# All taps of six channel tiles of a depthwise convolution on TensorE, as four output phases on 32-row blocks

## The reference

```python
TAPS = 31                                  # CONV_A_WIDTH; D_MODEL = 1024, SEQ = 512
def mixer_conformer_conv(x, w_pw1, b_pw1, w_dw, b_dw, ln_g, ln_b, w_pw2):
    a, g = jnp.split(x @ w_pw1 + b_pw1, 2, axis=-1)
    h = a * jax.nn.sigmoid(g)
    h = causal_depthwise_conv(h, w_dw) + b_dw       # 31 taps, one filter per channel
    h = jax.nn.silu(layer_norm(h, ln_g, ln_b))      # over the 1024 channels
    return h @ w_pw2
...
x = layer_norm(ALPHA * x + h, ln1_g[i], ln1_b[i])   # then a SwiGLU FFN, a second norm,
                                                    # and a gated per-layer embedding
```

## Time and profile before

| | |
|---|---|
| median of 3 runs | 2545.72 us (2544.5 to 2546.34) |
| the profiled execution's own time | 2546.59 us |
| its span | 2544.8 us |
| TensorE matmuls busy | 2520.1 us, 99% |
| TensorE weight loads busy | 2314.1 us, 91% |
| VectorE busy | 1955.3 us, 77% |
| ScalarE busy | 1200.0 us, 47% |
| mean granted TensorE clock | 0.999 |

### The profile page before, as it was taken

The page is one execution under the profiler, slowest core; times in us unless marked ns, Lnnn a source line. Parts: engine busy times, 40 slices in busy tenths (PEclk is TensorE's granted clock), DMA queues, the critical chain, the costliest instruction groups (busy, mean ns, idle before and its releaser), DMA issues. The chain is left out here.

```text
span 2544.8 us, 41246 instructions
## 1 busy us (share of the span) xinstructions
PE 2520.1 (99%) x17241; PEld 2314.1 (91%) x17241; DVE 1955.3 (77%) x2571; ACT 1200.0 (47%) x1960; POOL 1.4 (0%) x10
## 2 busy tenths in 40 slices
PE   9999999999999999999999999999999999999999
PEld 7899999889888899998898899998898999999888
DVE  6988999577454679995784479996677979999576
ACT  6775444436233254443362245444356766444335
POOL 0000000000000000000000000000000000000000
PEclk9999999999999999999999999999999999999999
DMA  5202333324322223333233224333222203333322
GB/s 156 73 12 92 113 103 108 103 88 128 95 92 91 84 89 103 107 101 108 82 101 97 94 67 123 103 108 107 92 91 93 66 26 97 103 107 102 108 82 76
DMA packets 267054, 240.10 MB, mean 94 GB/s; under 512 B 14908, under 2 KB 212852, under 8 KB 266740
## 3 DMA queue, kind: packets, MB, share of 16 engines
q1 hardware_dynamic: 266292, 236.94, 30.2%
q10 hardware_dynamic: 576, 0.52, 0.1%
HBM read 233.21 MB, written 2.10 MB: 92 GB/s over the span
## 5 line engine op out<-in xcount | busy, mean ns | idle before, releaser
L1786 DVE TENSOR_TENSOR w_lo<-raw,w_hi 128x1024 fp32r<-128x1024 f32 x287 | 345.4, 1222 | 266.0 <-ACT w_hi L1309 265.7
L1309 ACT CAST w_hi<-raw 128x1024 fp32r<-128x1024 f32 x287 | 294.8, 1045 | 372.8 <-DMA raw<-in_ffn_w_down_dram 104.1
L879 PE MATMUL psum<-h_hi,w_lo 128*128 128x512 f32 x872 | 341.4, 392 | 0.0
L881 PE MATMUL psum<-h_hi,w_hi 128*128 128x512 f32 x872 | 339.4, 389 | 0.0
L880 PE MATMUL psum<-h_lo,w_hi 128*128 128x512 f32 x856 | 333.2, 389 | 0.0
L1024 PE MATMUL psum<-a_hi,w_lo 128*128 128x256 f32 x1088 | 280.9, 286 | 6.6 <-DVE w_lo L1786 5.1
L1024 PE MATMUL psum<-a_hi,w_hi 128*128 128x256 f32 x1088 | 277.5, 284 | 0.0
L1190 PE MATMUL psum<-h_hi,w_hi 128*128 128x256 f32 x768 | 217.3, 283 | 0.0
L1191 PE MATMUL psum<-h_hi,w_hi 128*128 128x256 f32 x768 | 217.3, 283 | 0.0
L1024 PEld LDWEIGHTS psum<-a_hi,w_lo 128*128 128x128 f32 x1088 | 209.1, 192 | 8.7 <-DVE w_lo L1786 4.6
L1024 PEld LDWEIGHTS psum<-a_hi,w_hi 128*128 128x128 f32 x1088 | 209.3, 192 | 0.3
(11 more groups left out here) (362 smaller groups left out, 6494.3 us busy)
## 6 DMA issues: line engine op xcount, KB each, us to landing
raw<-in_ffn_w_gate_dram SPq DMA_DIRECT2D x176, 256.0 KB, 3.0
raw<-in_ffn_w_up_dram SPq DMA_DIRECT2D x176, 256.0 KB, 3.3
raw<-in_ffn_w_down_dram SPq DMA_DIRECT2D x176, 256.0 KB, 3.1
raw<-in_a_w_pw_dram SPq DMA_DIRECT2D x94, 256.0 KB, 3.1
raw<-in_ple_w_gate_dram SPq DMA_DIRECT2D x64, 256.0 KB, 3.2
raw<-in_b_w_in_dram SPq DMA_DIRECT2D x64, 256.0 KB, 3.0
raw<-in_c_w_in_dram SPq DMA_DIRECT2D x48, 256.0 KB, 2.9
raw<-in_b_w_out_dram SPq DMA_DIRECT2D x32, 256.0 KB, 3.1
```

Of the source, the lines that this page charges most:

```text
L879: pe.matmul(bank(grp.g, j), st_lo, mv_hi, start=(k == 0), stop=False, skip_group_check=by_tiles(grp))
L881: done = pe.matmul(bank(grp.g, j), st_hi, mv_hi, start=False, stop=(ku == last and a == UK - 1), skip_group_check=by_tiles(grp))
L1309: act.copy(hi_u[u % RING], raw_u[u % RING]).then_inc(hi_ready, 1)
L1786: dve.tensor_tensor(lo_u[u % RING], raw_u[u % RING], hi_u[u % RING].bitcast(F32), ALU.subtract)\
```

## The change

TensorE makes all 31 taps of six tiles (2 to 7); VectorE keeps tiles 0 and 1. Four output phases take the place of two: a matmul has 32 rows and 128 output columns (32 channels by four phases), the four row groups r go to four PSUM banks, and 31 taps and four phases give 34 steps. Tiles 2 to 5 are made over all 512 tokens (128 moving columns for each matmul); tiles 6 and 7 in two halves of the tokens (64 moving columns), in the order 6 and 7 of half 0, 6 and 7 of half 1. Successive segments alternate between the two halves of PSUM. The DMAs that moved quadrants are gone: ScalarE (`move`) and VectorE (`move_half`) copy 32-partition pieces out of PSUM, 16 copies by ScalarE for a whole tile, eight by each engine for half a tile. ScalarE makes the blocks of tiles 2 and 3, VectorE those of tiles 4 to 7 (`make_blocks`). The full diagonals, the taps of tiles 2, 3 and 7 on VectorE and the two ScalarE starts (`conv_begin`) are gone.

```diff
-PHASED = ((4, 0), (5, 0), (3, K_SHARED), (6, 0))
-TILE_ROWS = P // 2
+PHASES = 4
+ROWS = P // PHASES
+STEPS = TAPS_A + PHASES - 1
+QUADS = (2, 3, 4, 5, 6, 7)
+ACT_BLOCKS = 2
+A_BLOCKS = 3
+SEGMENTS = ((0, None), (1, None), (2, None), (3, None), (4, 0), (5, 0), (4, 1), (5, 1))
+CENTRE_IN, CENTRE_AT = 3, 20
+STATS_AT = 18
...
+        def moves(s, i, groups):
+            n, (v0, n_v) = SEGMENTS[i][0], segment_span(i)
+            y = by_phase(tiles(h_f32, CONV_Y + QUADS[n]))
+            return [(rows(y, r)[:, PHASES - 1 - j, v0:v0 + n_v], rows(segment_bank(s, i, r), j))
+                    for r in groups for j in range(PHASES)]
...
-            def phase_tap(s, n, e):
-                at = e % 2 * (CW // 2) + e // 2
-                for w, x in ((0, 1), (1, 0), (0, 0)):
-                    for r in range(2):
-                        moving = conv_split(n, x)[r * TILE_ROWS:(r + 1) * TILE_ROWS, at:at + HALF]
-                        last = pe.matmul(phase_bank(s, n, r)[:, 0:HALF], block_pair(n, e, w, r), moving, ...)
+            def quad_tap(s, i, e):
+                n, (v0, n_v) = SEGMENTS[i][0], segment_span(i)
+                at = e % PHASES * (CW // PHASES) + e // PHASES + v0
+                for w, x in ((0, 1), (1, 0), (0, 0)):
+                    for r in range(PHASES):
+                        moving = rows(conv_split(n, x), r)[:, at:at + n_v]
+                        block = rows(tap_blocks(n, w), r)[:, e * ROWS:e * ROWS + P]
+                        last = pe.matmul(segment_bank(s, i, r), block, moving, ...)
...
             def conv_taps(s):
+                for i, (n, h) in enumerate(SEGMENTS):
+                    if i < 2:
+                        take_half(s.taps_g + i)
+                    else:
+                        pe.wait_ge(moved_high, moved(s, i - 2))
+                        pe.wait_ge(moved_low, moved(s, i - 2))
+                    if i == CENTRE_IN + 1:
+                        pe.wait_ge(centre_saved, c + 1)
...
+                    for e in range(STEPS):
+                        last = quad_tap(s, i, e)
+                        if i == CENTRE_IN and e == CENTRE_AT:
                             centre(s)
+                        if i == len(SEGMENTS) - 1 and e == STATS_AT:
+                            conv_stats(s, 0)
                     last.then_inc(taps_done, 1)
...
             # ScalarE
+            def move(s, i):
+                act.wait_ge(taps_done, moved(s, i))
+                for y, out_of in moves(s, i, HIGH):
+                    last = act.copy(y, out_of)
+                last.then_inc(moved_high, 1)
+                if i < WHOLE:
+                    for y, out_of in moves(s, i, LOW):
+                        last = act.copy(y, out_of)
+                    last.then_inc(moved_low, 1)
...
             def conv_norm(s):
+                for i in (4, 5):
+                    move(s, i)
+                    conv_half_square(s, i)
+                move(s, 6)
+                load_sqrt()
+                half_moments(s, 0)
+                half_root(s, 0)
+                move(s, 7)
+                load_silu()
+                conv_half_square(s, 6)
+                half_affine_pair(s, 0, 0)
...
             # VectorE
+            def make_blocks(s, n):
+                if n >= A_BLOCKS:
+                    dve.wait_ge(pe_done, s.groups[-1].end())
+                m = QUADS[n]
+                for part in range(2):
+                    ...
+                    last = dve.tensor_tensor(three(tap_block(n, 0, part, TAPS_A), TAPS_A), many(rep[:, :], TAPS_A),
+                                             taps.broadcast_to([P, TAPS_A, ROWS]), ALU.mult)
+                last.then_inc(blocks_made, 1)
+            def move_half(s, i):
+                m, h = QUADS[SEGMENTS[i][0]], SEGMENTS[i][1]
+                dve.wait_ge(taps_done, moved(s, i))
+                for y, out_of in moves(s, i, LOW):
+                    last = dve.tensor_copy(y, out_of)
+                last.then_inc(moved_low, 1)
+                wait_moved(s, i)
+                place_centred(s, m, h)
...
             def conv_norm(s):
+                move_half(s, 4)
+                add_half(s, 4)
+                add_half_square(s, 4)
...
+                half_root(s, 0)
+                half_scale(s, 0, 0)
+                half_scale(s, 0, 1)
+                move_half(s, 7)
+                add_half_square(s, 6)
+                add_half(s, 7)
+                half_lo_pair(s, 0, 0)
```

More of the change, by code:

```diff
@@ L381, in tap_block @@
[L381 to L401, removed]
+            return ap.rearrange("p (q v) -> p q v", q=PHASES)
@@ L403, in prm_taps, with mean_bank, square @@
+        def mean_bank(s):
+            return bank(s.taps_g, 0, 2).rearrange("p (h s) -> p h s", h=2)[:, :, SEQ // PHASES:SEQ // PHASES + HALF]
+        SQUARES = DT + TILES
+        def square(m):
+            return tiles(a_f32, SQUARES + m - TILES)
         def prm_taps(s):
@@ L943, in last_tap @@
[L943 to L948, removed]
+                    for r in range(PHASES):
+                        moving = rows(conv_split(n, x), r)[:, at:at + n_v]
+                        block = rows(tap_blocks(n, w), r)[:, e * ROWS:e * ROWS + P]
+                        last = pe.matmul(segment_bank(s, i, r), block, moving, start=(e == 0 and (w, x) == (0, 1)),
+                                         stop=(e == STEPS - 1 and (w, x) == (0, 0)))
@@ L1902, in phase_add @@
-            def phase_add(s, n):
-                dve.wait_ge(phase_turned[n], 64 * (s.layer // 3 + 1))
-                own.settle()
-                y = by_phase(tiles(h_f32, CONV_Y + PHASED[n][0]))
-                own.add(dve.tensor_tensor(y, y, phased(turned(n)[1]), ALU.add))
-            def make_shared_blocks(s, part):
-                dve.wait_ge(pe_done, s.groups[-1].end())
-                m, n = PHASED[SHARED][0], TAPS_A - K_SHARED
-                taps = (taps_lo if part else prm_taps(s)).rearrange("p (k m) -> p k m", m=DT)[:, K_SHARED:TAPS_A, m:m + 1]
-                to = (h_hi, h_lo)[part][:, SHARED_AT + TILE_ROWS:SHARED_AT + (n + 1) * TILE_ROWS]
-                dve.tensor_tensor(three(to, n), many(rep, n), taps.broadcast_to([P, n, TILE_ROWS]), ALU.mult)\
-                   .then_inc(shared_blocks, 1)
@@ new lines, in add_half, with add_half_square @@
+            def add_half(s, i):
+                c, m, h = s.layer // 3, QUADS[SEGMENTS[i][0]], SEGMENTS[i][1]
+                last = i % 2 == 1
+                dve.wait_ge(z_ready, Z_READY * c + i + 2)
+                own.settle()
+                ins_ = dve.tensor_tensor(hcol(tiles(tmp, 5), h), hcol(tiles(tmp, 5), h), hcol(conv_tile(m), h), ALU.add)
+                ins_.then_inc(conv_sums, 1) if last else own.add(ins_)
+            def add_half_square(s, i):
+                c, m, h = s.layer // 3, QUADS[SEGMENTS[i][0]], SEGMENTS[i][1]
+                last = i % 2 == 1
+                dve.wait_ge(sq_ready, 7 * c + i)
@@ L2254, in convolve @@
                         lo_to(min(lo_end[0] + 1, lo_end_at))
-                    for m in (m0, m0 + 1) if k > first or not begun else ():
+                    for m in (m0, m0 + 1):
                         x = conv_x[:, m, PAD - taps + 1 + k:PAD - taps + 1 + k + SEQ]
@@ L2265, in convolve @@
                             own.add(dve.scalar_tensor_tensor(y, x, w, y, ALU.mult, ALU.add))
-            def tap_alone(s, m, k, y, fresh=False):
-                x, w = conv_x[:, m, k:k + SEQ], col("a_w_dw", s.layer // 3 * TAPS_A + k, m)
-                if fresh:
-                    own.add(dve.tensor_scalar(y, x, w, None, ALU.mult))
-                else:
-                    own.add(dve.scalar_tensor_tensor(y, x, w, y, ALU.mult, ALU.add))
-            def convolve_alone(s, m, first, end):
-                sums = tiles(h_f32, CONV_Y + m), tiles(tmp, 5)
-                for k in range(first, end):
-                    own.settle(back=1)
-                    tap_alone(s, m, k, sums[(k - first) % 2], fresh=(k == first + 1))
-                own.settle()
-                own.add(dve.tensor_tensor(sums[0], sums[0], sums[1], ALU.add))
             def gated_input(s, grp):
```

419 lines of the change are left out of this document (169 added, 250 removed).

## The result

The changed kernel takes 2712.73 us (median of 4 runs, 2710.82 to 2716.29) against 2545.11 us (2543.06 to 2546.34): a ratio of 1.0661, 95% interval 1.0643 to 1.068, or 167.6 us more. The profiled execution's span is 2709.0 us. The time lies in the range of the prediction and the direction is the one forecast; of the loss of 167.6 us the prediction had 76.

What follows compares the result with a forecast made beforehand. TensorE's matmuls, busy 99% of the span, were taken to bound the kernel. Two layers by (34.4 + 3.8) = 76.4 us on the profiled 2546.6 gave 2623.0, set at 2622 us as that execution was 0.9 above the median; range 2598 to 2740.

Steps and rivals of the forecast that it cites:

- Added on TensorE: Tap stages: 816 groups of four 32-row matmuls at 119.2 ns, 97.3 us, 34.4 us more than before in each layer.
- the same for 128 and for 64 columns: Sign expected in the new trace's taps: groups of four every 110 to 120 ns at either stream length.
- almost full clock: Reading of the profile before the change: TensorE's matmuls busy 99% of the span at nearly the full clock.
- The load bounds the group: Taps: if four row groups load and stream at once, the 128-column weight load sets a group's price, 109 to 119.2 ns.
- bounds 109 and 119.2: Price of a tap group in ns: bare distance between loads, and price of a 64-row pair, which was taken.
- The tail: Behind the taps: ScalarE's copies, table load and square before the first SiLU, 3.8 us of new TensorE idle time per layer.
- upper bound of 6.6 us: Most that the new idle time behind the taps could be; the least was 1.9 us.
- What was costed at nothing: VectorE's changed work, segments' waits for inputs, sums and banks, ScalarE's whole-tile copies and removed quadrant DMAs: no added time.
- The faster one: Rival for the taps: quarter-height loads faster or hidden, the stream decides; 16.5 us saved per layer, 2513 us; chance 0.13.
- Short streams at plain float32's rate: Rival for the taps: float32r under 256 columns about fourfold slower, 225 ns for 128 columns; 2708 us; chance 0.07.
- Slow instructions: Rival for the taps: eight instructions per group bound it, 2715 us at 22 ns each, up to 2817; chance 0.22.
- the likeliest case: Whole kernel: the forecast of load-bound groups plus idle time behind the taps, 2602 to 2634 us; chance 0.56.

Runs made afterwards that it cites:

- e1: The changed kernel with the half segments streaming all 128 columns, half of their results unused; 2637.1 us, ratio 1.0366.
- e10: The changed kernel with 32 unused words more, so later tensors lie where they lay before the change; 2690.8 us, ratio 1.0575.
- e6: On top of e5, tiles 3 to 6 run two passes as one 256-column matmul, two loads per step instead of three; 2579.6 us, ratio 1.0136.
- e3: On top of e1, ScalarE's SiLU table load and square of segment 6 stand before the last segment's copies; 2633.7 us, ratio 1.0349.
- e5: The changed kernel with all six tiles whole, 612 groups in place of 816, norm sums behind the taps; 2598.7 us, ratio 1.0209.
- e12: The shared-load kernel e6 with the 32 unused words of e10; 2558.1 us, ratio 1.0053.
- e7: The changed kernel with only the first two half segments streaming 64 columns, the last two 128; 2714.4 us, ratio 1.0663.
- e8: The changed kernel with the first two half segments streaming 128 columns, the last two 64; 2674.1 us, ratio 1.0503.
- e2: The changed kernel with whole segments also streaming 64 columns after each bank's first matmul, half their outputs left out; 2791.7 us, one run.
- e9: The changed kernel plus an unused group of four 256-column matmuls in each half-segment step, timed in rounds; median 2715.1 us, ratio 1.0646.

## Why the prediction was wrong

The loss of 167.6 us falls apart by differences of kernels that differ in one thing:

| | us |
|---|---|
| clock at 1.2 GHz through short streams (changed kernel less e1) | 75.6 |
| tensors 128 bytes off (changed kernel less e10) | 21.9 |
| what is left over, taken as the terms that the prediction had | 70.1 |
| predicted for these | 76.4 |

The third line is a remainder. The traces bear it out: the stages of taps take 94.0 and 97.1 us in e1, where they took 64.5 and 64.8 before, and 3.9 us of idle time come in each layer, together 69.6 us.

**What failed** is the step "Added on TensorE", where one price read at 2.4 GHz was taken for all 816 groups. It said "the same for 128 and for 64 columns", which the trace confirms at either level, 112 and 213 ns; but the prediction read "almost full clock" off as a property of the kernel and had no case in which its own change moves it. Some 364 groups of layer 0 and 373 of layer 3 (2949 matmuls that start while the clock is low) ran at 213 ns instead of 112: 737 by 0.101 = 74 us. That a matmul queue busy without a gap can lose the clock was nowhere in the earlier trace rows, since no row there has fewer than 256 columns. The Trainium skill, in the same page on TensorE, section "Part 1: The HAM clock gate (the "warmup" mystery)", says that the clock gate follows how busy TensorE has been. The trace has a fall while the profile calls the engine 99% busy, so that share is not a reading of what the gate goes by; the rule would have been a rival worth a chance.

**What was missing** is a term for the place of the tensors. It was in the diff as one line of an allocation, and it touches 4800 matmuls of 512 columns in all layers, 5.3 ns on each of 3744 and 4.1 on 1056, 24 us by that sum where e10 gives 21.9.

**What held, by its steps.** The load bounds the group, and four row groups load at once: for it speak the unchanged spacing at 149.08 and e6, where two loads for three make 0.23 for 0.34 us. Both would come out the same if each instruction took 14 ns to issue, eight of them 112 ns, and no run changes the one without the other. Against that, the four loads of a group start within 0.01 us of each other (in the changed kernel and in e1), and two loads of full height stand 0.11 us apart with two instructions between the starts, not eight. Its price was 112 ns; of the bounds 109 and 119.2 I took the wrong end, 816 by 0.007 = 6 us too much in each layer. The tail: 4.68 us idle for 4.6, and e3 moved 3.4 us of it for 3.6 expected. (Its upper bound of 6.6 us adds up to 6.5.) It had a second cost, not foreseen: even in e1 the clock goes down for 6.8 us in this idle time, and the first products behind it run at half speed. What was costed at nothing stayed hidden: TensorE's matmuls pause at no start of a segment. The only pause in the taps of layer 0 is 0.18 us inside segment 1, at 114.86, and segment 3 takes 0.63 us more than segment 0, for the centre.

**The rivals.** The faster one fell with the load's price. Short streams at plain float32's rate fell too: 128 columns cost 112 ns, not 225, and 64 columns cost the same. Slow instructions, priced midway at 2715 us, came within 2 us of the time and are false all the same: the eight instructions of a group of four fit into 112 ns at full clock, and e1 issues as many of them as the changed kernel and is 75.6 us faster. A time that agrees with a rival says nothing; the spacing under either clock does. That the range holds the time is luck of the same kind: the likeliest case ended at 2634 us, and what lies above it was there for slow instructions and short streams at plain float32's rate. Neither happened; a fall of the clock, which did, was given no chance.

**The expectations that missed.** e5 (2571) and e6 (2541) were set before the shift was known; some 22 us of their 28 and 39 are that. For e6, e12 shows it (21.5 us); e5 was not run with the pad. The rest is put down to the tail, with 16 us in e6 where 10 were allowed, and to half clock around it. e12's 13 us over the kernel before are by the same account that tail against 8.6 us of shorter taps in each layer; no run takes the tail away. No version here beats the kernel before. One that halves the last tile's copies and shares loads was not built: in e6 ScalarE's 16 copies of 32x128 take 6.9 us and the staging 1.4 more, together over the 7.9 us of such a segment. Whether it would have paid is open.

## What to carry to other kernels

When a change makes streams much shorter than their weight loads (64 columns here), price its matmuls at both clock levels, and read the clock by windows over the changed stage; a busy share of 99% doesn't say which level. A stream lengthened to no other use can be worth it: half of e1's columns in the halves are waste, and it is 75.6 us faster. After any change of allocations compare the spacing of matmuls in a stage that the change doesn't touch; if it moved, restore the offsets before anything else is judged.

## What the runs showed of the hardware that was not expected

- The granted clock fell from 2.4 to 1.2 GHz while TensorE issued loads and matmuls with no pause over 0.3 us (none in layer 0 of the changed kernel), 1.7 to 4.9 us behind the start of the first 32-row groups of 64 columns (e7 1.7, e8 2.2 and 4.3, changed kernel 4.2 and 4.9, e2 4.9). It never fell in the stages of 128-column groups (e1, e5), nor in those of e6.
- Groups of 128 columns keep the level that they find: up in e1, down in e7 for 45.6 us.
- At 1.2 GHz the loads start 213 ns apart, where they start 112 ns apart at 2.4 GHz, with 64 columns (changed kernel) and with 128 (e7).
- Steps of mixed streams, three groups of 64 columns and one of 256, gave 2693.6 to 2731.8 us from one kernel (e9).
- Four row groups of 32 rows load and stream at once, also 256 columns: a group of 256 and one of 128 take 0.23 us together (e6).
- A shift of 128 bytes in SBUF changes the spacing of 512-column float32r matmuls from 227 to 233 ns on average; matmuls that stream from a tensor ahead of the shift kept 227.
- A copy of 32x128 costs ScalarE 0.39 us out of PSUM and 0.43 out of SBUF (16 in 6.27 and in 6.9 us, e6), of 32x64 out of PSUM 0.27 us (eight in 2.17, changed kernel), so moving quadrants by copies is dear in pieces.
